# Projection of the sample frames: one stationary tile with the high and low halves side by side, two matmul passes for three, and the halves added at eviction

## The reference, cut to what matters

```
h = rms_norm(x, norm_mix_gain)          # (1024 + 64 frames) x 1024
h @ w_in                                # 1024 x 5136 columns
```

## Time and profile before

| | |
|---|---|
| time, median of 3 runs | 1719.93 us (1717.57 to 1723.35) |
| the profiled execution's own time | 1721.89 us |
| its span (first to last instruction in the trace) | 1719.2 us |
| PE busy in the span | 1597.7 us (93%) |
| mean granted TensorE clock | 0.969 of full |
| end of the first stage (first SP issue of the second) | 787.33 us |
| main-column matmuls, lines 956 to 958 | 2160, 305.5 + 283.5 + 284.5 us busy |

### The profile page before, as it was taken

One profiled execution on the slowest core, in us unless ns is written; L12 is line 12 of the kernel. 1 busy time (PEld: TensorE's weight loads), 2 busy tenths in 40 slices (PEclk: granted clock), 3 DMA queues, 4 the chain that ended last, 5 costly groups with the idle time before them and its releaser, 6 DMA issues.

```text
span 1719.2 us, 23126 instructions
## 1 busy us (share of the span) xinstructions
PE 1597.7 (93%) x8247; PEld 1304.3 (76%) x8247; DVE 1042.1 (61%) x1247; ACT 766.0 (45%) x812; POOL 565.2 (33%) x452
## 2 busy tenths in 40 slices
PE   7999999999999999995899995699999999999993
PEld 6888787778877778884688884478878787777772
DVE  5211355565655425444455555788888888888885
ACT  4310332332332332214222213477777777777773
POOL 2311354342553404320001011243344344344334
PEclk9999999999999999997899997799999999999997
DMA  6221432332230404327333333699999999999986
GB/s 220 99 92 68 127 117 77 117 96 68 62 117 31 138 35 153 117 97 274 130 110 110 129 148 151 232 366 361 362 371 369 362 375 366 370 372 373 367 297 233
DMA packets 111808, 346.39 MB, mean 201 GB/s; under 512 B 15996, under 2 KB 44844, under 8 KB 86016
## 3 DMA queue, kind: packets, MB, share of 16 engines
q1 hardware_dynamic: 101312, 327.08, 51.6%
q0 software_dynamic: 10432, 18.45, 4.1%
HBM read 301.90 MB, written 65.34 MB: 214 GB/s over the span
## 4 chain that ended last, share of the span: by engine, by line
PE 25%; DMA 13%; POOL 4%; DVE 4%; issue 4%; ACT 2%; SPq 1%; POOLq 0%; ACTq 0%
DMA x_nat<-h_mid,gather_at 6%; DMA we_raw<-in_w_experts 5%; PE banks_ffn L1777 2%; PE banks_ffn L1779 2%; PE banks_ffn L1778 2%; DVE we_lo L1939 2%; PE banks_ffn L1285 2%; PE banks_ffn L1287 2%; PE banks_ffn L1286 2%; POOL x_mid L2024 2%; PE banks_ffn L1272 2%; PE banks_ffn L1273 2%; PE banks_ffn L1274 2%; PE banks_ffn L1279 1%; PE banks_ffn L1795 1%
## 5 line engine op out<-in xcount | busy, mean ns | idle before, releaser
L1939 DVE TENSOR_TENSOR we_lo<-we_raw,we_hi 128x2048 fp32r<-128x2048 f32 x192 | 432.7, 2288 | 56.5 <-ACT we_hi L1842 53.3
L1842 ACT ACTIVATE we_hi<-we_raw 128x2048 fp32r<-128x2048 f32 x186 | 352.9, 1916 | 88.9 <-PE banks_ffn L1779 72.8
L956 PE MATMUL p_bank<-w_hi,ht_hi 128*128 128x512 f32 x720 | 305.5, 424 | 2.4 <-DVE ht_lo L723 1.6
L958 PE MATMUL p_bank<-w_hi,ht_lo 128*128 128x512 f32 x720 | 284.5, 395 | 0.0
L957 PE MATMUL p_bank<-w_lo,ht_hi 128*128 128x512 f32 x720 | 283.5, 394 | 0.0
L1777 PE MATMUL banks_ffn<-we_hi,x_hi 128*128 128x512 f32 x512 | 207.3, 405 | 2.9 <-DVE x_lo L1943 2.9
L924 POOL TENSOR_TENSOR beta<-beta,prod 128x512 f32<-128x512 f32 (+3 forms) x120 | 131.7, 1110 | 217.5 <-DVE prod L776 217.5
L1779 PE MATMUL banks_ffn<-we_hi,x_lo 128*128 128x512 f32 x512 | 201.6, 394 | 0.0
L1778 PE MATMUL banks_ffn<-we_lo,x_hi 128*128 128x512 f32 x512 | 200.8, 392 | 0.0
L776 DVE TENSOR_TENSOR_SCAN prod<-keep,prod 128x512 f32<-128x512 f32 (+3 forms) x120 | 128.8, 1103 | 83.8 <-ACT keep L631 78.7
L719 DVE COPY stage<-p_bank 128x512 f32<-128x512 f32 x90 | 61.9, 688 | 172.1 <-PE p_bank L958 171.8
(11 more groups left out here) (325 smaller groups left out, 2743.2 us busy)
## 6 DMA issues: line engine op xcount, KB each, us to landing
we_raw<-in_w_experts SPq DMA_DIRECT2D x192, 1024.0 KB, 11.0
projected<-stage SPq DMA_DIRECT2D x90, 256.0 KB, 2.0
w_raw<-in_w_main SPq DMA_DIRECT2D x80, 256.0 KB, 4.8
gates<-projected SPq DMA_DIRECT2D x9, 1024.0 KB, 4.9
qkvr<-projected SPq DMA_DIRECT2D x9, 768.0 KB, 5.6
o_nat<-mixed SPq DMA_DIRECT2D x9, 512.0 KB, 3.3
x_mid<-x_new SPq DMA_DIRECT2D x9, 512.0 KB, 2.9
h_mid<-h_new SPq DMA_DIRECT2D x9, 512.0 KB, 2.6
```

The source lines that it names most:

```text
L956: pe.matmul(out, ht_hi[:, k, rows], w_hi[:, j], start=(k == 0), stop=False)
L958: last = pe.matmul(out, ht_lo[:, k, rows], w_hi[:, j], start=False, stop=(k == KD - 1))
L1842: act.activation(w_hi[:, j], w_raw[:, j], ACT.Copy).then_inc(high[j], 1)
L1939: dve.tensor_tensor(w_lo[:, j], w_raw[:, j], w_hi[:, j].bitcast(F32), ALU.subtract).then_inc(split[j], 1)
```

## The change

The 64 sample frames are half of a tile. The new kernel writes the low halves of these frames into the columns that held zeros, so that `ht_hi[:, k, 1024:1152]` is 64 high columns and 64 low columns. One pass with `w_hi` gives hi·hi in PSUM partitions 0 to 63 and lo·hi in 64 to 127; a second pass with `w_lo` adds hi·lo to the first 64 (and lo·lo to the others). Eviction then adds the two halves: a copy of partitions 64 to 127 to the stage, a wait for it, and an addition of partitions 0 to 63. The third rank group does the same with columns for partitions. Only 64 rows are stored; the zero rows of `projected`, which later loads read, are written once at the start by five DMAs. The planner's costs of slices change, and with them the order in the other queues.

```diff
@@ put_slices
-            put("slice", g, k, cost=0.68 if width_of(g) == N else 0.36)
+            put("slice", g, k, cost=0.45 if groups[g][1] == SAMPLE else 0.68 if width_of(g) == N else 0.25)
@@ tiles and semaphores
-        ht_lo = sb("ht_lo", [P, KD, ROWS], F32R)
+        ht_lo = sb("ht_lo", [P, KD, SEQ], F32R)
+        KEPT = 16 * (1 + MAIN // D)
@@ SP
             sp.dma_start(io["x_rows"][SEQ:ROWS, :], x_in[:, SAMPLE]).then_inc(x_kept, 16)
+            for c in range(MAIN // D):
+                sp.dma_start(io["projected"][SEQ + DEC:ROWS, columns(c, D)], x_in[DEC:P, SAMPLE]).then_inc(x_kept, 16)
...
-                    sp.dma_start(io["projected"][rows_of(t), columns(ORDER[pos], N)], stage[:, j]).then_inc(stored[j], 16)
+                    h = DEC if t == SAMPLE else P
+                    sp.dma_start(io["projected"][t * P:t * P + h, columns(ORDER[pos], N)], stage[0:h, j]).then_inc(stored[j], 16)
...
                         wait_stored(sp, QUICK * TILES)
+                        sp.wait_ge(x_kept, KEPT)
@@ ACT
-            act.activation(ht_hi[:, :, rows_of(t)], turned_x[t % 2], ACT.Copy).then_inc(ht_high, 1)
+            n = DEC if t == SAMPLE else P
+            act.activation(ht_hi[:, :, t * P:t * P + n], turned_x[t % 2][:, :, 0:n], ACT.Copy).then_inc(ht_high, 1)
...
-            act.wait_ge(x_kept, 16)
+            act.wait_ge(x_kept, KEPT)
@@ DVE, evacuate
             if ORDER[pos] == RANKS:
+                if t == 2:
+                    out = s.rank_t[:, SEQ:SEQ + DEC]
+                    dve.tensor_copy(out, p_bank[0:RANK, g % BANKS, DEC:P]).then_inc(rank_folded, 1)
+                    dve.memset(s.rank_t[:, SEQ + DEC:ROWS], 0.0).then_inc(rank_folded, 1)
+                    dve.wait_ge(rank_folded, 2)
+                    dve.tensor_tensor(out, p_bank[0:RANK, g % BANKS, 0:DEC], out, ALU.add).then_inc(evacuated, 1)
+                    return
...
+            if t == SAMPLE:
+                out = stage[0:DEC, j % STAGES]
+                dve.tensor_copy(out, p_bank[DEC:P, g % BANKS]).then_inc(folded, 1)
+                dve.wait_ge(folded, len([b for b in store_of if b <= g and groups[b][1] == SAMPLE]))
+                dve.tensor_tensor(out, p_bank[0:DEC, g % BANKS], out, ALU.add).then_inc(evacuated, 1)
+                return
@@ DVE, ht_low_part
+            if t == SAMPLE:
+                dve.tensor_tensor(ht_hi[:, :, SEQ + DEC:ROWS], turned_x[t % 2][:, :, 0:DEC],
+                                  ht_hi[:, :, SEQ:SEQ + DEC].bitcast(F32), ALU.subtract).then_inc(ht_low, 1)
+                return
@@ PE, multiply
+            if ORDER[pos] == RANKS and t == 2:
+                out, rows = p_bank[:, g % BANKS, 0:P], rows_of(SAMPLE)
+                pe.matmul(out, w_hi[:, j, 0:P], ht_hi[:, k, rows], start=(k == 0), stop=False)
+                last = pe.matmul(out, w_lo[:, j, 0:P], ht_hi[:, k, rows], start=False, stop=(k == KD - 1))
+            elif t == SAMPLE:
+                out, rows = p_bank[:, g % BANKS], rows_of(SAMPLE)
+                pe.matmul(out, ht_hi[:, k, rows], w_hi[:, j], start=(k == 0), stop=False)
+                last = pe.matmul(out, ht_hi[:, k, rows], w_lo[:, j], start=False, stop=(k == KD - 1))
```

More of the change, by code:

```diff
@@ L393, in mix_in @@
         x_loaded = [sem(f"x_loaded{t}") for t in range(TILES)]
-        x_zeroed, x_kept = sem("x_zeroed"), sem("x_kept")
+        x_zeroed, x_kept, folded, rank_folded = sem("x_zeroed"), sem("x_kept"), sem("folded"), sem("rank_folded")
         squared, rooted, normed = sem("squared"), sem("rooted_mix"), sem("normed")
@@ L582, in _ @@
             wait_stored(sp, CHUNKS * TILES)
-            sp.wait_ge(x_kept, 16)
+            sp.wait_ge(x_kept, KEPT)
             sp.wait_ge(o_stored, 16 * PAIRS)
@@ L947, in multiply @@
             j = n % SLICES
-            if ORDER[pos] == RANKS:
+            if ORDER[pos] == RANKS and t == 2:
[6 more added lines that the diff above has]
+                last = pe.matmul(out, ht_hi[:, k, rows], w_lo[:, j], start=False, stop=(k == KD - 1))
+            elif ORDER[pos] == RANKS:
                 width = width_of(g)
```

## The result

The change makes the kernel faster, by less than forecast. Medians, taken on one chip: 1721.56 us before (1717.45 to 1723.35, 8 runs), 1712.66 after (1708.68 to 1714.85, 8 runs). The ratio is 0.9948, interval 0.9934 to 0.9961, a gain of 8.9 us where 14.5 was forecast, and the median lies 0.7 us above the range.

A forecast was written before the change was run, and what follows sets the result against it. PE's list of matmuls was taken to bound the first stage, with GpSimd nearly late. 19.0 - 1.9 - 0.7 - 0.35 - 0.55 - 1.05 = 14.5 us gain, so 1719.93 becomes 1705.4 us; range 1701 to 1712.

The forecast's parts named there:

- The gross price: Matmuls removed from ten sample groups (18.1 us) and the third rank group (0.9 us): 19.0 us before anything is given back.
- The boundaries: First three chunk boundaries: of 5.4 us saved, 3.5 stay and 1.9 are given back to waits for weights.
- loads put ahead of a store: Second and third boundaries: new costs put the second load ahead of a store, speaking for the upper gain of 1.9 us.
- Group 35: Attention: PE's transpose waits behind GpSimd's back-to-back work; 0.7 us given back (0 to 1.2).
- the slower rival: Clock stays at its low level for a whole group at four boundaries: 19 us lost, 1724 us; chance 0.04.
- Groups 44, 53 and 65: Sample groups found without a GpSimd queue like group 35's; each keeps its full 1.81 us.
- the second operation: Added eviction operation, nine sample groups before the last: costs PE nothing, as the bank is needed 5.44 us later.
- the rank groups: Transpose at 491.29 us waits behind GpSimd's subtractions: 0.35 of the 0.9 us saved is given back.
- the recurrence: Groups 74 and 83, where masks, roots and `w_lo` follow closely: 0.55 us given back (0 to 1.2).
- The end: Last group's two-operation eviction and last output behind its store: 0.75 of 1.81 us stays, 1.05 given back.
- More waits than I found: Rival: GpSimd pins every sample group up to the sixth; 7.5 us gain or fewer, 1712.5 to 1717 us; chance 0.11.
- lowest case: Boundaries keep only 1.3 us; group 35 gives back 0.5 more, the recurrence 0.65, the end 0.25: gain 10.9 us.

The follow-up runs named there:

- a1: The changed kernel with the planner's old costs, so the other four queues keep the order of the kernel before: 1713.45 us, ratio 0.9957 to the kernel before.
- a3: The kernel before with the planner's new costs and nothing else: 1721.48 us, ratio 1.0003 to the kernel before.
- b3: The changed kernel with thirteen weight slots for twelve: 1710.29 us, ratio 0.9924 to the kernel before.
- the second execution: The changed kernel profiled once more, with no edit: 1714.21 us in one run.
- d1: The changed kernel with group 44's eviction behind VectorE's two `weight_t` copies and the last store behind the last gated output: 1711.47 us, ratio 0.9942 to the kernel before.
- a2: The changed kernel with one copy as eviction of a sample group, the addition of the other half left out: 1708.74 us, ratio 0.9929 to the kernel before.
- a4: The kernel before with the third pass left out of the ten sample groups and third rank group, all else unchanged: 1711.41 us, ratio 0.9945 to the kernel before.
- e1: The changed kernel with three of GpSimd's products for beta moved ahead of subtractions near 475 to 484 us: 1706.64 us, ratio 0.9914 to the kernel before.
- e3: The kernel before with the last two products for beta moved ahead of subtractions near 484 us: 1717.77 us, ratio 0.9983 to the kernel before.
- d2: The changed kernel with thirteen weight slots, group 44's eviction and the last store both moved later: 1708.6 us, ratio 0.9917 to the kernel before.
- e2: The changed kernel with thirteen slots, both later steps, beta products moved near 475 to 484 us and one near 252: 1702.05 us, ratio 0.9894 to the kernel before.

## Why the prediction missed

**Right.** The gross price: a sample group is 3.62 us, 24 matmuls to 16 at 0.2267. The boundaries: 3.5 forecast; without the start's share 3.69 and 3.37 measured, waits for `w_lo` at the places named. The agreement is partly luck: what is given back at the three was forecast as 0.8, 1.6 and 1.5 and came out as 0.8, 0.9 and 1.95. The argument from loads put ahead of a store holds, as a1 and a3 show. b3 shows that a weight slot was what was short, though it doesn't separate loading from subtracting. Group 35 and the wait for beta in 36, "about 1 us": 0.91. Groups 53, 65 and 83. The eviction as two operations of 0.7. The clock stays at its 2.4 GHz level through the boundaries (1.00 from 60 to 180 us, where the longest wait is 1.06), so the slower rival found nothing to stand on there. The prediction took this from the earlier trace rows, which doesn't show it: its window, 129 to 172 us, lies between two boundaries and holds no wait. The Trainium skill, TensorE: Matmul & The Clock Gate, § What's actually happening, has activity release a throttle that is the default; no wait at a boundary was enough to bring it back here, while a wait of 1.80 us, the one ahead of 484.07, was, in eight of the eleven executions that have it.

**Wrong: "Groups 44, 53 and 65 I find without such a queue and cost at their full 1.81".** For 44 that is false by 1.25 us (0.98 in the second execution). I looked at GpSimd's queue and not at VectorE's. The error begins at "Those two waits name the one engine that is nearly late: GpSimd": the same list of waits had 1.4 us on VectorE's `weight_t`, which I passed over as small change beside 0.8 us for `w_lo`. Shown by d1: the same operations in another order, and the group gives 1.93.

**Wrong: "In the other nine sample groups the second operation costs PE nothing: PE needs the bank again a whole group, 5.44 us, later".** The bank isn't what is waited for. Behind the eviction in VectorE's queue stands other work that PE wants sooner. By a2 against after the operation costs 2.1 us, 0.7 of it at the end, which was forecast.

**Mis-sized: the rank groups**, 0.35 given back of 0.9. All of it was, as GpSimd's path of 16.56 us has the same length in both kernels. I counted which slices lie ahead of one scoring step; the saving is taken at the waits behind it too. a4 shows that the fold's operations have no part in it, e1 and e3 that GpSimd's order is the cause.

**Mis-sized: the recurrence**, 0.55 given back for two groups. Group 83 gave its 1.64. Group 74 gave 0.10: PE, no longer held by 5.4 us of matmuls, waits for the mask. In a1 this is the whole loss, 1.06 us. The other 0.65 are the late `w_lo` and the late mix step behind it, and they have no single cause: a1, with the added operations and the old order of the queues, gave 0.75, a2, without them and with the new order, 0.64, and a4, with neither, 0.77. Only the two together brought it to 0.10 and, in the second execution, -0.07; but the five other kernels with both gave 0.27 to 0.54, so timing has a part. The prediction cost the reordering, "two roots ahead of subtractions" among it, at 0. No edit was made for this place.

**Missed: the clock at ends**, 1.36 us, in both executions of the changed kernel. The prediction considered the clock only where a wait would be new. Here no wait is new. Twelve kernels show two lengths: 5 to 8 slow matmuls (before, a1, a3, d1, e1, e3) or 10 to 12 (after, a2, a4, b3, d2, e2). The long form costs 1.6 us (-1.36 to -1.39 against +0.22 to +0.25 between the two columns), and each of the two kernels run twice kept its own. The records show where the forms part: in the seven traces of the long form the granted clock falls 3.0 to 3.5 us after the first narrow matmul, while they still run, and in the seven of the short form 3.6 to 4.9 us after it. What decides when it falls stays open: no edit of mine was made for it, and d1 and d2 differ only in the slots, far ahead of it.

**The end**: 0.75 forecast, 0.33 measured. The addition is 0.68, as taken, but the store of 64 partitions takes 0.47 us to issue and the last output behind it 0.58, where the earlier trace rows have 0.33 and 0.34.

Together: 1.25 + 0.57 + 1.36 + 1.43 + 0.42 lost and 0.13 at group 65, 0.17 at 35, less 0.3 won at the boundaries and 0.1 at 83, is 4.9 of the 5.0 us by which 14.5 exceeds 9.52. Against the 8.4 us of the averaged executions 1.1 us more are missing, most of which is the slower start and boundaries of the profile before. The rival "More waits than I found" is the one that came closest, but it placed them on GpSimd in groups 9 to 53. The range was too narrow below: its lowest case let only the four named places give back more, and had nothing for a queue of VectorE's inside the attentions.

## What to carry to other kernels

When an engine that is always busy loses work, list for each place what it reaches next and look at the queue of every engine that must deliver it: an item there costs when it stands ahead of what is awaited, whatever its own result is needed for. An operation added to an engine that is half empty is then cheap or dear by its place in the queue, and the place is a free edit: 1.4 us for one eviction moved by two positions, 5 us for three products moved past subtractions that nobody was waiting for. Memory that a change frees is worth spending at once on the wait that the change makes (here one weight slot, 2.5 to 3.9 us at the boundaries), and a profile before should be taken twice, as two executions were 1.8 us apart at the first scoring step, over half of it from the start. What the start has given or taken must come off before places behind it are compared.

## What the runs showed of the hardware

**Half a store is no faster.** The medians over all stores mislead here: 3.0 us to landing for the ten of 128 KB against 2.0 for the eighty of 256 KB. The sample's stores go out when weights are loaded, and in the kernel before the same ten, of 256 KB, take 3.6. At group 44 nothing slows the store: before, it lands as fast as the median of the others. Its row in the list of DMA issues (KB, us to landing), before and after:
```profile
projected<-stage SPq DMA_DIRECT2D x1, 256.0 KB, 2.0
...
projected<-stage SPq DMA_DIRECT2D x1, 128.0 KB, 2.3
```
128 KB from 64 partitions land 2.27 us after the issue begins, 256 KB from 128 partitions after 2.04, and the issue itself takes 0.50 against 0.34 us; at the last group it is 2.36 against 2.01, with 0.47 against 0.33. The Trainium skill, SBUF — State Buffer, § Door 1: The DMA port swizzle, gives 64 partitions half of the ports, by which both would take equally long; apart from the longer issue that is so here, to 0.2 us.

**A wait of 1.8 us may or may not drop the clock.** Of the kernels whose PE waits 1.8 us for beta near 480 us, before, after (both executions each), a1, a2 and d2 ran 4 to 6 of the wide matmuls behind it at 0.43 us, with a granted clock of 0.50, d1 two, and a3, a4 and b3 none, with the clock at 1.00 and nearly the same instructions around it.
